# Seven block products for the up tiles of every second pair, with a new order of splits and sums on the vector engine

## What is computed

```python
def half_ffn(x, g, w_gate, w_up, w_down):
    h = rmsnorm(x, g)
    return 0.5 * ((jax.nn.silu(h @ w_gate) * (h @ w_up)) @ w_down)
...
x = x + half_ffn(x, ...)      # D_MODEL = 1024, D_FF = 2816, float32
```

## Time and profile before

| | before |
|---|---|
| median of 3 runs | 2202.9 us (2197.45 to 2203.23) |
| the profiled execution | 2199.94 us, of it 2198.3 us span |
| TensorE (PE) busy | 2129.5 us, 97% |
| VectorE (DVE) busy | 1352.5 us, 62% |
| ScalarE (ACT) busy | 861.6 us, 39% |
| chain that ended last | PE 87%, DVE 7%, ACT 3%, issue 3% |
| mean granted TensorE clock | 0.985 |

### The profile page before, as it was taken

The page is one execution under the profiler, slowest core; times in us unless marked ns, Lnnn a source line. Parts: engine busy times, 40 slices in busy tenths (PEclk is TensorE's granted clock), DMA queues, the critical chain, the costliest instruction groups (busy, mean ns, idle before and its releaser), DMA issues.

```text
span 2198.3 us, 42097 instructions
## 1 busy us (share of the span) xinstructions
PE 2129.5 (97%) x17908; PEld 2070.3 (94%) x17908; DVE 1352.5 (62%) x2124; ACT 861.6 (39%) x1232; POOL 67.2 (3%) x140
## 2 busy tenths in 40 slices
PE   7899999999988999999999999999999999999998
PEld 7899999999978899999999999999997599999997
DVE  6763675686455557737656754675657547745754
ACT  5431332344244444313334332333457634322323
POOL 0000000100100000000000000000102300000000
PEclk9999999999998999999999999999999999999999
DMA  4332232533200333332323232332324423232321
GB/s 148 89 103 83 84 106 70 132 83 85 75 10 2 82 91 97 106 92 87 95 79 115 78 106 87 106 92 82 102 78 131 140 78 106 78 110 82 113 74 64
DMA packets 318362, 199.16 MB, mean 91 GB/s; under 512 B 10006, under 2 KB 313266, under 8 KB 318168
## 3 DMA queue, kind: packets, MB, share of 16 engines
q1 hardware_dynamic: 309840, 174.49, 27.0%
q0 software_dynamic: 6160, 19.84, 3.1%
q10 hardware_dynamic: 2176, 2.15, 0.3%
HBM read 188.52 MB, written 8.05 MB: 89 GB/s over the span
## 4 chain that ended last, share of the span: by engine, by line
PE 87%; DVE 7%; ACT 3%; issue 3%; DMA 0%; ACTq 0%; DVEq 0%
PE PS L2505 60%; PE PS L2526 17%; PE PS L2678 4%; DVE wlo L1608 1%; PE PS L3220 1%; ACT whi L959 1%; PE PS L3139 1%; PE PS L3153 0%; DVE ht_l L1692 0%; PE PS L3122 0%; ACT xb L1020 0%; DVE tmp L1665 0%; DVE X L2052 0%; PE PS L3205 0%; PE PS L3023 0%
## 5 line engine op out<-in xcount | busy, mean ns | idle before, releaser
L2505 PE MATMUL PS<-hb_h,whi 128*128 128x260 f32 x2448 | 498.2, 285 | 1.8 <-DVE hb_l L2430 1.8
L2505 PE MATMUL PS<-hb_h,wlo 128*128 128x260 f32 x2448 | 496.1, 284 | 0.0
L2505 PE MATMUL PS<-hb_l,whi 128*128 128x260 f32 x2448 | 493.9, 283 | 0.0
L2505 PEld LDWEIGHTS PS<-hb_h,whi 128*128 128x128 f32 x2448 | 380.7, 189 | 4.5 <-DVE wlo L1608 1.4
L2505 PEld LDWEIGHTS PS<-hb_h,wlo 128*128 128x128 f32 x2448 | 378.7, 189 | 0.0
L2505 PEld LDWEIGHTS PS<-hb_l,whi 128*128 128x128 f32 x2448 | 377.5, 189 | 0.0
L1608 DVE TENSOR_TENSOR wlo<-stage,whi 128x1024 fp32r<-128x1024 f32 (+1 forms) x193 | 232.6, 1205 | 151.1 <-ACT whi L959 145.5
L959 ACT ACTIVATE whi<-stage 128x1024 fp32r<-128x1024 f32 (+1 forms) x193 | 199.9, 1038 | 123.3 <-PE PS L2526 64.4
L1608 DVE TENSOR_TENSOR wlo<-stage_x,whi 128x1024 fp32r<-128x1024 f32 (+1 forms) x148 | 175.1, 1185 | 52.2 <-ACT whi L959 51.9
L959 ACT ACTIVATE whi<-stage_x 128x1024 fp32r<-128x1024 f32 (+1 forms) x148 | 150.8, 1022 | 133.4 <-DVE stage_x L1600 115.2
L1813 DVE SCALAR_TENSOR_TENSOR tmp<-PS,rstd 128x520 f32<-128x520 f32 x64 | 44.7, 698 | 235.8 <-PE PS L2505 235.8
(11 more groups left out here) (472 smaller groups left out, 3764.2 us busy)
## 6 DMA issues: line engine op xcount, KB each, us to landing
stage<-in_ffn_w_up SPq DMA_DIRECT2D x88, 512.0 KB, 3.8
stage_x<-in_ffn_w_gate SPq DMA_DIRECT2D x36, 1024.0 KB, 5.2
stage<-in_w_in_e SPq DMA_DIRECT2D x28, 512.0 KB, 3.8
stage_x<-in_ffn_w_down SPq DMA_DIRECT2D x20, 512.0 KB, 4.2
stage<-in_ffn_w_down SPq DMA_DIRECT2D x40, 256.0 KB, 2.7
stage<-in_w_in_o SPq DMA_DIRECT2D x20, 512.0 KB, 3.8
stage<-in_ffn_w_gate SPq DMA_DIRECT2D x16, 512.0 KB, 3.8
stage_x<-in_ffn_w_down SPq DMA_DIRECT2D x20, 384.0 KB, 3.7
```

The lines of the kernel that those rows point to most:

```text
L2505: mm = pe.matmul(psum[:, half, :], w, x(k, half), start=first and w is hi and x is rhs_hi, stop=last and w is lo)
```

## The change

Up becomes a group in pairs 2, 4, 6, 8 and 10 too (`"SS"`). `P2` goes ahead of `P6` in the order. The splits of the next group's batches are spread over the events as before, counted on from its own (`own`). The seven sums of a group's results become five: one for `c11` and `u2` together while the products run (over two banks, with the copied `P1` taken twice), and four after the seventh product, the last again over two banks. The finishing of both tiles moves behind the seventh product. In the head the token sums come first in a gate unit, ahead of the splits and of the read of the gate's PSUM; the low half `ht_l` moves from the up unit to the gate unit, and ACT's silu behind `ht_h`. PE's `P7` and `P4` wait for the first of the five sums.

```diff
-MODES = ("PP", "PP") + ("SP",) * 9
+MODES = ("PP", "PP") + ("SS", "SP") * 4 + ("SS",)
-ORDER = ("P1", "P6", "P2", "P5", "P3", "P7", "P4")
+ORDER = ("P1", "P2", "P6", "P5", "P3", "P7", "P4")
...
-        U2_SUM, C11_SUM, V_SUM, C12_SUM, U3_SUM, C22_SUM, C21_SUM = range(1, 8)
+        P1_SUMS, U3_SUM, V_SUM, C12_SUM, C2_SUMS = range(1, 6)
...
 # ACT
                 def head(n, up, done):
-                    ahead(done - 1)
                     if not up:
-                        silu(n)
                         act.wait_ge(x_ready, KD * (s + 1))
...
                         act.activation(xb[:], xT[:, 2 * n, :], ACT.Copy, scale=h_scale(s, 2 * n)).then_inc(t_act, 1)
-                    else:
+                    ahead(done - 1)
+                    if not up:
                         act.wait_ge(t_dve, 5 * (KP * f + n) + 4)
                         act.activation(ht_h[:, :, n, :], snapT[:], ACT.Copy).then_inc(t_act, 1)
+                        silu(n)
+                    else:
                         high(n)
...
                     elif which == "P7":
                         ahead(done, own + 3)
+                    elif which == "P4":
                         half_of(2 * t, up)
-                    elif which == "P4":
                         late.append((2 * t + 1, up))
...
 # DVE
+                def token_sums(n):
...
                 def head(n, up, done):
+                    if not up:
+                        token_sums(n)
                     ahead(done - 1)
...
                         take(two(tmp[:, n % 2, :]), pair(2 * (n % 2))).then_inc(gate_read, 1)
...
+                        dve.wait_ge(t_act, X_TURNED + 2 * (KP * f + n) + 2)
+                        dve.tensor_tensor(ht_l[:, :, n, :], snapT[:], ht_h[:, :, n, :].bitcast(F32), ALU.subtract)\
                            .then_inc(t_dve, 1)
...
-                    elif which == "P2":
+                    elif which == "P6":
                         reach(done)
-                        if q:
-                            dve.wait_ge(block_sum, BLOCK_SUMS * q)
                         dve.wait_ge(p1_copied, q + 1)
-                        add(q, U2_SUM, u2, p1, bank["P6"])
...
-                        add(q, C11_SUM, c11, p1, bank["P2"])
+                        add(q, P1_SUMS, tile0, PS[:, first + 1:first + 3, 0:HALF], p1.to_broadcast([P, 2, HALF]))
                         ahead(done, own)
...
                     elif which == "P4":
                         reach(done)
-                        add(q, C21_SUM, c21, u3, bank["P4"])
+                        add(q, U3_SUM, snapT[:, 1, :], PS[:, bank_of("P7", up), 0:HALF], c12, P1_SUMS)
+                        add(q, V_SUM, c12, PS[:, bank_of("P5", up), 0:HALF], c12, U3_SUM)
+                        add(q, C12_SUM, c12, PS[:, bank_of("P3", up), 0:HALF], c12, V_SUM)
+                        dve.wait_ge(act_lo if up else prod_ready, base + 2 * t)
+                        add(q, C2_SUMS, tile1, PS[:, first + 2:first + 4, 0:HALF], u3.to_broadcast([P, 2, HALF]))
+                        half_of(2 * t, up, q)
                         half_of(2 * t + 1, up, q)
...
 # PE
-                    elif which == "P7":
-                        pe.wait_ge(block_sum, BLOCK_SUMS * q + U2_SUM)
-                    elif which == "P4":
-                        pe.wait_ge(block_sum, BLOCK_SUMS * q + C11_SUM)
+                    elif which in ("P7", "P4"):
+                        pe.wait_ge(block_sum, BLOCK_SUMS * q + P1_SUMS)
```

More of the change, by code:

```diff
@@ L350, in bank_of @@
         def bank_of(which, up):
-            return 4 * up + {"P1": 0, "P6": 1, "P2": 2, "P5": 3, "P3": 0, "P7": 1, "P4": 2}[which]
+            return 4 * up + {"P1": 0, "P2": 1, "P6": 2, "P5": 3, "P3": 0, "P7": 1, "P4": 2}[which]
         def act_slot(n):
@@ L1037, in group_step @@
                         ahead(done, own)
-                        if late:
-                            half_of(*late.pop())
+                    elif which == "P6" and late:
+                        half_of(*late.pop())
                     elif which == "P5":
@@ L1685, in product @@
                        .then_inc(prod_ready, 1)
+                def token_sums(n):
+                    count, x1, g1 = 5 * (KP * f + n), xT[:, 2 * n + 1, :], h_scale(s, 2 * n + 1)
+                    t1, t2, t3, t4 = (snapT[:, m, :] for m in range(4))
+                    b11, b12, b21, b22 = xb[:, 0:HALF], xb[:, HALF:TOK], x1[:, 0:HALF], x1[:, HALF:TOK]
+                    dve.wait_ge(t_act, X_TURNED + 2 * (KP * f + n) + 1)
+                    if count:
+                        dve.wait_ge(t_dve, count)
+                    dve.tensor_tensor(t1, b12, b11, ALU.subtract).then_inc(t_dve, 1)
+                    dve.scalar_tensor_tensor(out=t3, in0=b22, scalar=g1, in1=b12, op0=ALU.mult, op1=ALU.subtract)\
+                       .then_inc(t_dve, 1)
+                    dve.wait_ge(t_dve, count + 1)
+                    dve.scalar_tensor_tensor(out=t2, in0=b22, scalar=g1, in1=t1, op0=ALU.mult, op1=ALU.subtract)\
+                       .then_inc(t_dve, 1)
+                    dve.wait_ge(t_dve, count + 3)
+                    dve.scalar_tensor_tensor(out=t4, in0=b21, scalar=g1, in1=t2, op0=ALU.mult, op1=ALU.subtract)\
+                       .then_inc(t_dve, 1)
                 def head(n, up, done):
+                    if not up:
+                        token_sums(n)
                     ahead(done - 1)
[L1690 to L1693, removed]
                     reach(done)
@@ L1740, in group_step @@
                     own = BY_FIRST[f, g, "a"].n + (6 if MODES[t][1] == "P" else 4)
-                    bank = {w: PS[:, bank_of(w, up), 0:HALF] for w in PRODUCTS}
-                    u2, u3, p1 = (snapT[:, n, :] for n in range(3))
-                    (c11, c12), (c21, c22) = ([tmp[:, a + 2 * up, h * HALF:(h + 1) * HALF] for h in range(2)] for a in range(2))
+                    first = 4 * up
+                    u3, p1 = snapT[:, 1:2, :], snapT[:, 2:3, :]
+                    tile0, tile1 = two(tmp[:, 2 * up, :]), two(tmp[:, 2 * up + 1, :])
+                    c12 = tmp[:, 2 * up, HALF:TOK]
                     if which == "P1":
                         ahead(done, own - 1)
-                    elif which == "P2":
+                    elif which == "P6":
                         reach(done)
-                        if q:
-                            dve.wait_ge(block_sum, BLOCK_SUMS * q)
                         dve.wait_ge(p1_copied, q + 1)
-                        add(q, U2_SUM, u2, p1, bank["P6"])
                         if base + 2 * t >= 2:
                             dve.wait_ge(act_lo if up else prod_ready, base + 2 * t - 1)
-                        add(q, C11_SUM, c11, p1, bank["P2"])
+                        add(q, P1_SUMS, tile0, PS[:, first + 1:first + 3, 0:HALF], p1.to_broadcast([P, 2, HALF]))
                         ahead(done, own)
@@ L1760, in group_step @@
                     elif which == "P3":
[L1761 to L1764, removed]
                         ahead(done, own + 2)
                     elif which == "P7":
[L1767 to L1770, removed]
                         ahead(done, own + 3)
```

6 lines of the change are left out of this document (3 added, 3 removed).

## The result

The changed kernel takes 2211.6 us (median of 5 runs, 2209.25 to 2214.94), the kernel before 2200.4 beside it; the ratio is 1.005, 95% interval 1.0035 to 1.0065. The span of the profiled execution went from 2198.3 to 2209.9 us, 11.6 more.

The account below looks back on a forecast made before the run. PE was taken to bound the kernel, with DVE having time to spare. 2199.9 less 28.8 (products) and 19.7 (head), plus 57.6 (new waits) and 6 (clock), gave 2215 us; forecast range 2207 to 2225, chance 0.55.

Parts of the forecast that it names:

- Products: Five up pairs in each of four stages, 12 matmuls less each: 28.8 us less, all on the path.
- Head: PE's four waits for `ht_l`: 14.4 us less waiting and 5.3 less half clock, together 19.7 us less.
- DVE behind a pair of two groups: PE's `P3` and `P7` wait for ACT's copy and DVE's first sum: 14.4 us a stage, 57.6 us more.
- the two bounds, 0.62 and 0.90: DVE's sum over two banks: one 520-column instruction, 0.62 us (taken), or two dependent ones of 260, 0.90.
- DVE's share, forecast at over nine tenths: Sign of the forecast: DVE busy for over nine tenths of a pair of two groups.
- The clock in the new waits: Behind pairs 2, 4 and 8, twelve places: clock falls at half, about 1.0 us each, 6 us more.
- a sign of being wrong: The forecast would be wrong if, among other signs, the clock fell at all of the new waits or none.
- The bounds, 0 and 21.6: Range for the clock's cost in the new waits, up to 12 falls of 1.8 us.
- The sum: Whole kernel: 2199.9 - 28.8 - 19.7 + 57.6 + 6 = 2215 us.
- That DVE comes in time: Rival: DVE's waiting steps run as fast as others from up sums to next gate sum; 2191 us, chance 0.08 (with 2151).
- the case of no change: Rival: waits as summed, no fall of the clock, steps 1 to 3% shorter; 2200 to 2208 us, chance 0.20.
- That the sums over two banks cost 0.90: Part of the dearer rival: about 1.2 us more at sixteen places, 19 us; 2230 to 2250, chance 0.17.

Follow-up runs that it names:

- e2_copy_first: The changed kernel with ACT's copy of `P1` moved ahead of the silu or high part of the tile before it: 2207.2 us, ratio 1.0032 to the kernel before.
- e5_own_waits: The changed kernel with added DVE waits on its own queue, between splits and between a group's two finishings: 2218.2 us, ratio 1.0082 to the kernel before.
- e9_old_head: The changed kernel with the head put back as in the kernel before, on ACT and DVE: 2230.9 us, ratio 1.0152 to the kernel before.
- e6_all_up: The changed kernel with copy of `P1` and first sum moved earlier, and up a group in all nine pairs behind the head: 2245.2 us, ratio 1.0208.

## Why the prediction was right

**Products.** 240 matmuls less, 28.8 us, as summed; at full clock a group still takes 10.08 us.

**Head.** Summed 14.4 of waits and 5.3 of half clock, 19.7. Measured by the starts: the first group of the first stage came 3.84 earlier (75.92 in the earlier trace rows to 72.08), the heads of the others were 4.42, 2.10 and 4.42 shorter, 14.8 together; three first groups ran at full clock, 1.6 each, 4.9. That is 19.7 again, but only because 0.4 us too little in the waits and 0.4 too much in the clock cancel, which is luck. The first stage kept 2.9 us of its wait (3.1 forecast) and its half clock.

**DVE behind a pair of two groups.** The steps added from the earlier trace rows hit the places almost exactly: for the second stage, whose first group starts at 847.60, they put the copy at 27.67 and the first sum at 30.21, that is 875.27 and 877.81; the trace has 875.27 and 877.76. A sum over two banks lasts 0.69 us and the next step starts 0.61 after it (877.76 to 878.37 in the trace), so that of the two bounds, 0.62 and 0.90, the lower was right. What three groups lost by pair, against the forecast, in the second stage (pair 10 has two):

| pair | forecast, us | measured, us |
|---|---|---|
| 2 | 3.6 | 3.65 |
| 4 | 4.2 | 4.25 |
| 6 | 1.6 | 1.76 |
| 8 | 4.2 | 4.51 |
| 10 | 0.8 | 1.00 |

Pair 8 stands out by 0.26 in this stage alone, and no run tells why. With 14.9 to 15.2 in each stage this is 60 us for 57.6. The parts were off by a little against each other: from the time it was due, `P3` came 1.57 us late and `P7` 1.28, for 1.72 and 1.42 forecast, and what the second matmul behind each stop comes later (0.1), which the sum hadn't, made up for it. DVE's share, forecast at over nine tenths, was 83% over the three groups and 90% in its own stretch there, from its first sum in pair 2 at 852.11 to the end of that in pair 3 at 878.45 (23.78 us of 26.34).

**The clock in the new waits.** This step failed: 6 us were taken, a fall at half of twelve places, and there was none at any, which the forecast itself had named as a sign of being wrong. The bounds, 0 and 21.6, held it. The runs show the falls elsewhere: one wait of 2.50 us brought them at eight of twelve places in `e2_copy_first`, waits of 1.40 and 1.12 with a stretch of products between them at none of twelve here. What decides it at one place, no run shows.

**The sum** with what was measured: 2199.9 - 28.8 - 19.7 + 60.2 = 2211.6, which is the profiled execution's time. The 3.4 us between forecast and result are the clock's 6, less 2.6 by which the waits were put too low. That these two misses have opposite signs is luck; without the clock's term the forecast would have been 2209, 2.6 too low.

**The rivals.** That DVE comes in time hung on steps that wait running at the pace of those that don't; the sums in the trace still start 0.46 us after one another where they wait, and `e5_own_waits` shows the price directly. Of the case of no change one half came, no fall of the clock, and the other not, steps 1 to 3% shorter than their rows. That the sums over two banks cost 0.90 was wrong. The forecast put the loss down to the order of steps in DVE's and ACT's queues and was right on that, but it looked at the two new waits as a price of the up groups; the runs show that they were a price of the order, and that 45 of the 60 us could be had back by moving a copy and a sum.

## What to carry to other kernels

Where an engine's queue holds a short step that the bound engine waits for behind a step that waits for a third engine, ask what the short step really needs and put it first: here a copy of 0.4 us and a sum of 0.7 cost 45 us. Remove such waits together, since each covers the other; one alone gave nothing on ACT, where the longer wait that was left brought the clock down. Adding a chain's steps from start to start in program order, with the waits between engines, gave a loss to within 5%, where DVE's busy share (67%) said that there was room.

## What was not expected of the hardware

In this kernel two short stops were cheaper than one of their length together. PE's clock stayed at 1.00 behind all twelve pairs of waits of 1.40 and 1.12 us with 1.4 us of products between, behind the same twelve in `e9_old_head`, and behind twelve of 1.63 to 1.99 and 1.12 in `e5_own_waits`. It fell to 0.50 behind eight of twelve single waits of 2.50 us, at 1.3 to 1.5 us each, and behind 10 of 24 of 2.0 in `e6_all_up`. The length of a wait doesn't settle it: in the kernel before it fell behind one of 1.94, and behind the same wait in `e9_old_head` it held (the wait, then the 3.5 us behind it):

```profile
1235.65 0.39 PE L2521 MATMUL PS<-hb_h,whi 128*128 128x260 f32 x1 [1.95 <-DVE ht_l L1692]
```

```profile
1235.65:1239.15 3.50, 3.50 (x29) 3.50 (x30) 1.25 (x2) 2.39 (x4) 0.00 (x0) 1.00 0.88 294
```

Why it holds in one place and falls in another, no run here tells. And a wait on the own queue on DVE cost 0.2 us between steps of 520 and 1024 columns, against 0.1 between sums of 260.
